# Sparse attention by pairs of heads with the values stationary, and additions to x one tile ahead

## What is computed

```python
def mixer_b(h, w_in, q_gain, k_gain, w_out, bias_tab):
    q, k, v, q_idx, k_idx, w_idx = split_last(h @ w_in, B_SPLITS)
    q = rms_norm(q.reshape(B, S, B_HEADS, HEAD_DIM), q_gain)
    k = rms_norm(k.reshape(B, S, B_KV_HEADS, HEAD_DIM), k_gain)
...
        sc = jnp.einsum('bqhd,bsd->bqhs', qib, k_idx).astype(jnp.float32) * (B_IDX_DIM ** -0.5)
        score = jnp.einsum('bqh,bqhs->bqs', wb.astype(jnp.float32), jax.nn.relu(sc))
        score = jnp.where(causal[None], score, -jnp.inf)
        _, sel = lax.top_k(score, topk)
...
        logits = jnp.einsum('bqhgd,bqkhd->bqhgk', qg, ks).astype(jnp.float32) * (HEAD_DIM ** -0.5)
        logits = jnp.where(valid[:, :, None, None, :], logits + bias, -jnp.inf)
        p = jax.nn.softmax(logits, axis=-1)
        o = jnp.einsum('bqhgk,bqkhd->bqhgd', p.astype(vs.dtype), vs)
...
    return out @ w_out
```

## Time and profile before

| | us |
|---|---|
| median of 3 runs | 3229.18 (3228.82 to 3231.17) |
| profiled execution | 3230.55 |
| its span | 3228.7 |
| PE busy | 3043.1 (94%) |
| DVE, ACT, POOL busy | 1073.0, 1108.9, 1371.6 |
| mean granted clock | 0.946 of full |

### The profile page before, as it was taken

The page is one execution under the profiler, slowest core; times in us unless marked ns, Lnnn a source line. Parts: engine busy times, 40 slices in busy tenths (PEclk is TensorE's granted clock), DMA queues, the critical chain, the costliest instruction groups (busy, mean ns, idle before and its releaser), DMA issues.

```text
span 3228.7 us, 37198 instructions
## 1 busy us (share of the span) xinstructions
PE 3043.1 (94%) x14352; PEld 2432.1 (75%) x14352; DVE 1073.0 (33%) x2072; ACT 1108.9 (34%) x1684; POOL 1371.6 (42%) x1097
## 2 busy tenths in 40 slices
PE   7999769999989989999899999899999999779999
PEld 5977558888656668888677787688888977558887
DVE  3023541113373341112656555311122133531112
ACT  4233432223343332223333434322334333332222
POOL 3455524454442224444433333244445355524443
PEclk8999889999985589999999999999999999889999
DMA  4222112323320012233311111122323222112332
GB/s 122 72 59 59 40 40 91 104 91 98 78 69 20 20 43 91 92 96 99 86 40 40 40 40 40 40 92 93 102 91 93 65 59 59 40 52 92 95 100 78
DMA packets 280064, 227.59 MB, mean 70 GB/s; under 512 B 30229, under 2 KB 275733, under 8 KB 279941
## 3 DMA queue, kind: packets, MB, share of 16 engines
q1 hardware_dynamic: 269200, 216.29, 22.4%
q10 hardware_dynamic: 10740, 9.65, 1.3%
HBM read 223.61 MB, written 2.30 MB: 70 GB/s over the span
## 4 chain that ended last, share of the span: by engine, by line
PE 83%; DVE 8%; POOL 4%; ACT 3%; issue 1%; DMA 0%; ACTq 0%; DVEq 0%; POOLq 0%
PE bank L1738 43%; PE bank L1681 22%; POOL w_lo L600 3%; PE bank L1758 3%; PE bank L1783 2%; PE bank L2081 1%; PE bank L2093 1%; PE bank L2090 1%; PE bank L1806 1%; PE bank L1771 1%; ACT w_hi L719 1%; POOL arena L622 1%; PE bank L1887 1%; PE bank L1905 1%; DVE rs L1327 1%
## 5 line engine op out<-in xcount | busy, mean ns | idle before, releaser
L600 POOL TENSOR_TENSOR w_lo<-raw,w_hi 128x512 fp32r<-128x512 f32 x808 | 1067.0, 1351 | 1385.4 <-ACT w_hi L719 1385.4
L719 ACT ACTIVATE w_hi<-raw 128x2048 fp32r<-128x2048 f32 x202 | 385.5, 1909 | 430.8 <-PE bank L1738 423.3
L1738 PE MATMUL bank<-h_hi,w_hi 128*128 128x512 f32 x1024 | 403.8, 394 | 0.0
L1738 PE MATMUL bank<-h_lo,w_hi 128*128 128x512 f32 x1024 | 400.7, 391 | 0.0
L1738 PE MATMUL bank<-h_hi,w_lo 128*128 128x512 f32 x1024 | 400.7, 391 | 0.0
L1738 PE MATMUL bank<-g_hi,w_hi 128*128 128x512 f32 x1024 | 398.3, 389 | 0.0
L1738 PE MATMUL bank<-g_lo,w_hi 128*128 128x512 f32 x1024 | 398.3, 389 | 0.0
L1738 PE MATMUL bank<-g_hi,w_lo 128*128 128x512 f32 x1024 | 398.3, 389 | 0.0
L1681 PE MATMUL bank<-h_hi,w_hi 128*128 128x512 f32 x784 | 339.7, 433 | 6.9 <-POOL w_lo L600 4.6
L1681 PE MATMUL bank<-h_lo,w_hi 128*128 128x512 f32 x784 | 316.7, 404 | 0.0
L1681 PE MATMUL bank<-h_hi,w_lo 128*128 128x512 f32 x784 | 316.3, 403 | 0.0
(11 more groups left out here) (245 smaller groups left out, 4591.7 us busy)
## 6 DMA issues: line engine op xcount, KB each, us to landing
raw<-in_mlp_w SPq DMA_DIRECT2D x128, 1024.0 KB, 5.3
raw<-in_a_w_in SPq DMA_DIRECT2D x48, 512.0 KB, 5.1
raw<-in_c_w_in SPq DMA_DIRECT2D x32, 512.0 KB, 5.6
raw<-in_a_w_in SPq DMA_DIRECT2D x12, 1024.0 KB, 5.0
raw<-in_b_w_in SPq DMA_DIRECT2D x18, 256.0 KB, 4.2
raw<-in_a_w_out SPq DMA_DIRECT2D x4, 1024.0 KB, 5.6
raw<-in_b_w_in SPq DMA_DIRECT2D x4, 1024.0 KB, 6.1
arena<-bias_scratch ACTq DMA_DIRECT2D x16, 256.0 KB, 3.1
```

Of the source, the lines that this page charges most:

```text
L600: ins = nc.gpsimd.tensor_tensor(w_lo[s][:, k, :], raw[s][:, k, :], w_hi[s][:, k, :].bitcast(F32), ALU.subtract)
L719: nc.scalar.activation(w_hi[s][:], raw[s][:], ACT.Copy).then_inc(w_hi_done, 1)
L1738: mm = nc.tensor.matmul(lin_bank[j][:], w[s][:, c, P * j:P * j + P], a[:, c, :], start=c + z == 0, stop=c == CT - 1 and z == 2)
```

## The change

In the sparse layer's attention a unit is now a block of queries for both heads of a pair: 32 units. The scores of the two heads use the two halves of the array's rows and banks 2 and 3; logits are negated, as in the dilated layers, so that one reduction gives the minimum and the exponential takes it as its bias. Transposes of the two heads go to banks 4 and 5, copied by ACT and DVE. In the weighing 64 columns of V are stationary and the probabilities stream, 128 columns at a time; bank 6 takes a whole pair, already transposed. The sums of a pair are inverted at once, spread over 64 partitions by eight matmuls with the identity, copied by ACT and multiplied in on DVE. Logits have four buffers, copied probabilities three. The scores of the next unit wait until both heads' logits of the last are done. POOL's mask additions take both heads at once.

The output projection is cut by heads: two chunks for the first eight heads, two for the others, four tiles of 12 matmuls in each. The first 96 matmuls run eight a step from step 21 on, 18 more in the two steps after the last unit. x so gets 16 additions instead of 8.

In the projections, keys come before queries, index scores are issued in twos, their relus have six buffers and the squares two, and the last five selection rounds stand behind the last addition of eps. In `residual` DVE adds tile c+1 to x before it makes the low part and the sum of tile c, in all layers.

```diff
+B_ORDER = (3, 0, 2, 1)
+B_UNITS = B_PAIRS * NB
+B_EARLY = (21, 8)
...
-            chunks += [("bq", i, c, CT, 4) for c in range(4)] + [("bk", i, 0, CT, 1)]
-            chunks += [("out", i, k, CT, 4) for k in range(4)]
+            chunks += [("bk", i, 0, CT, 1)] + [("bq", i, c, CT, 4) for c in range(4)]
+            chunks += [("bo", i, k, 4, 2) for k in range(4)]
...
+        bpt = [part(2 * TOK).rearrange("p (h n) -> p h n", h=2) for _ in range(3)]
+        btm = [part(2 * TOK).rearrange("p (h n) -> p h n", h=2) for _ in range(2)]
...
+        INDEX_AT = {(0, z): 2 * z for z in range(4)}
+        INDEX_AT.update({(2 + z // 2, 2 * (z % 2)): 8 + 2 * z for z in range(4)})
+        INDEX_AT.update({(6 + z // 2, 2 * (z % 2)): 16 + 2 * z for z in range(4)})
...
+            first, share = B_EARLY
+            return max(0, share * (s - first)), max(0, min(96, share * (s - first + 1)))
...
+                    t, n = b_masked(u), P * (b + 1)
...
+                    if t >= 2:
+                        pool.wait_ge(l_done, 2 * (4 * ((t - 2) // 3) + (0, 2, 3)[(t - 2) % 3] + 1))
+                    nc.gpsimd.tensor_tensor(btm[t % 2][:, :, 0:n], bbias[f % 2][:, :, TOK - n:TOK],
+                                            score[b].unsqueeze(1).to_broadcast([P, 2, n]), ALU.add).then_inc(tm_done, 1)
...
+                for u in range(B_UNITS):
+                    f, z, b = b_unit(u)
+                    if b:
+                        masked(u)
+                    for n in (chunk_at["bo", i, 0], chunk_at["bo", i, 1]):
+                        if u >= 2 and any(t + 1 == tile0[n + 1] for _, t in b_ended(i, u - 2)):
+                            split_ahead(n)
...
+                def probs(u):
+                    f, z, b = b_unit(u)
+                    for half in range(2):
+                        act.wait_ge(l_done, 2 * u + half + 1)
+                        t = bl[u % 4][:, half, 0:P * (b + 1)]
+                        c = 2 * b + half
+                        nc.scalar.activation(t, t, ACT.Exp, bias=b_stat(f, 0)[:, c:c + 1], scale=-1.0,
+                                             accum_out=b_stat(f, 1)[:, c:c + 1]).then_inc(p_done, 1)
...
+                def copy_turned(u):
+                    n = P * (b_unit(u)[2] + 1)
+                    act.wait_ge(pt_done, 2 * u + 1)
+                    if u >= 3:
+                        act.wait_ge(pv_done, u - 2)
+                    nc.scalar.activation(bpt[u % 3][:, 0, 0:n], bank[4][:, 0:n], ACT.Copy).then_inc(pt_copied[0], 1)
...
+                for s in range(B_UNITS + 6):
+                    f, z = divmod(s, NB)
+                    if 2 <= s < B_UNITS + 2:
+                        copy_turned(s - 2)
+                    if s < B_UNITS:
+                        if z == 1 and 1 <= f < B_PAIRS - 1:
+                            load_bias(f + 1)
+                        probs(s)
+                    if z == 2 and f:
+                        act.wait_ge(rinv_spread, f)
+                        act.wait_ge(y_done, f - 1) if f > 1 else act.wait_ge(qk_ready, Q + 10)
+                        nc.scalar.activation(brs, stat_bank[:], ACT.Copy).then_inc(rinv_copied, 1)
+                    if z == 3 and f:
+                        act.wait_ge(y_done, f)
+                        nc.scalar.activation(g_hi[:, f - 1, :], byf, ACT.Copy).then_inc(yh_done, 1)
+                    for n, t in b_ended(i, s - 1):
+                        if t + 1 == tile0[n + 1]:
+                            round_ahead(n)
...
-                for c in range(CT):
-                    dve.wait_ge(lin_done, t0 + c + 1)
-                    nc.vector.tensor_tensor(x[:, c, :], x[:, c, :], lin_bank[(t0 + c) % 2][:], ALU.add).then_inc(x_added, 1)
-                    if m is not None:
-                        dve.wait_ge(x_added, x0 + c + 1)
-                        low_x(m, c)
-                        sum_square(m, c)
+                for c in range(CT + 1):
+                    if c < CT:
+                        dve.wait_ge(lin_done, t0 + c + 1)
+                        nc.vector.tensor_tensor(x[:, c, :], x[:, c, :], lin_bank[(t0 + c) % 2][:],
+                                                ALU.add).then_inc(x_added, 1)
+                    if m is not None and c:
+                        dve.wait_ge(x_added, x0 + c)
+                        low_x(m, c - 1)
...
+                def logits(u):
+                    f, z, b = b_unit(u)
+                    n = P * (b + 1)
...
+                    if b:
+                        dve.wait_ge(tm_done, b_masked(u) + 1)
+                    else:
+                        dve.wait_ge(bbias_loaded[f % 2], 32 * (f // 2 + 1))
+                    dve.wait_ge(s_done, u + 1)
+                    for half in range(2):
+                        bias = btm[b_masked(u) % 2][:, half, 0:n] if b else bbias[f % 2][:, half, TOK - n:TOK]
+                        c = 2 * b + half
+                        nc.vector.tensor_tensor_reduce(
+                            out=bl[u % 4][:, half, 0:n], in0=bank[2 + half][:, 0:n], in1=bias, scale=1.0,
+                            scalar=-TAKEN, op0=ALU.add, op1=ALU.min,
+                            accum_out=b_stat(f, 0)[:, c:c + 1]).then_inc(l_done, 1)
...
+                    dve.wait_ge(p_done, 8 * f + 8)
+                    nc.vector.reciprocal(b_stat(f, 2), b_stat(f, 1)).then_inc(rinv_done, 1)
...
+                def outputs(f):
+                    dve.wait_ge(pv_done, 4 * f + 4)
+                    dve.wait_ge(rinv_copied, f + 1)
+                    nc.vector.tensor_tensor(by_block(byf), reversed_blocks(bank[6][:]), reversed_blocks(brs),
+                                            ALU.mult).then_inc(y_done, 1)
...
+                index_sums(range(8))
+                beside = {2: ((3, 0, 7),), 3: ((3, 7, 11),), 4: ((3, 11, 15),), 5: ((3, 15, 16),), 6: ((2, 0, 5),),
+                          7: ((2, 5, 10),), 8: ((2, 10, 14),), 9: ((2, 14, 16), (1, 0, 1)), 10: ((1, 1, 6),),
+                          11: ((1, 6, 11),)}
+                for k in range(2, 12):
+                    for b, lo, hi in beside[k]:
+                        if (b, lo) == (1, 0):
+                            index_sums(range(20, 24))
+                        for r in range(lo, hi):
+                            top(b, (r,))
+                    if k in (2, 5, 7):
+                        p = {2: 8, 5: 12, 7: 16}[k]
+                        index_sums(range(p, p + 4))
+                    add_eps(1, Q + k - 2, k >= 4)
+                top(1, range(11, 16))
...
+                for s in range(B_UNITS + 6):
+                    f, z = divmod(s, NB)
+                    if z == 3 and f:
+                        outputs(f - 1)
+                    if s < B_UNITS:
+                        logits(s)
+                    if 2 <= s < B_UNITS + 2:
+                        copy_turned(s - 2)
+                    if z == 0 and 0 < f <= B_PAIRS:
+                        inverses(f - 1)
+                    if z == 0 and f >= 2:
+                        low(f - 2)
+                    for n, t in b_ended(i, s):
+                        j = t - tile0[chunk_at["bo", i, 0]]
+                        dve.wait_ge(lin_done, t + 1)
+                        nc.vector.tensor_tensor(x[:, j, :], x[:, j, :], lin_bank[t % 2][:], ALU.add).then_inc(x_added, 1)
 
...
+                def scores(u):
+                    f, z, b = b_unit(u)
+                    if u:
+                        pe.wait_ge(l_done, 2 * u)
+                    for half in range(2):
+                        r = slice(HD * half, HD * half + HD)
+                        mm = nc.tensor.matmul(bank[2 + half][:, 0:P * (b + 1)], bq[f][r, P * b:P * b + P],
+                                              bk[f // 4][r, 0:P * (b + 1)], start=True, stop=True)
+                    mm.then_inc(s_done, 1)
+                def turn(u):
+                    b = b_unit(u)[2]
+                    for half in range(2):
+                        pe.wait_ge(p_done, 2 * u + half + 1)
+                        if u:
+                            pe.wait_ge(pt_copied[half], u)
+                        for k in range(b + 1):
+                            c = slice(P * k, P * k + P)
+                            mm = nc.tensor.transpose(bank[4 + half][:, c], bl[u % 4][:, half, c], ident)
+                        mm.then_inc(pt_done, 1)
+                def weigh(u):
+                    f, z, b = b_unit(u)
+                    if u == 0:
+                        pe.wait_ge(copied, copy_first[i] + 8)
+                    if z == 0 and f:
+                        pe.wait_ge(y_done, f)
+                    for half in range(2):
+                        pe.wait_ge(pt_copied[half], u + 1)
+                    for k in range(b + 1):
+                        for half in range(2):
+                            c = (2 * (f // 4) + half) * HD
+                            mm = nc.tensor.matmul(bank[6][HD * half:HD * half + HD, P * b:P * b + P], bv[:, k, c:c + HD],
```

(33 more changed lines are left out.)

470 lines of the change are left out of this document (133 added, 337 removed).

## The result

The changed kernel takes 3088.1 us in the median (3086.1 to 3091.7), against 3229.0 for the kernel before: a ratio of 0.9564, 95% interval 0.9547 to 0.9580, or 141 us less. The profiled execution took 3086.1 us with a span of 3084.3. The forecast was 3086, with a range of 3066 to 3120. From one profiled execution to the other it is 144.4 us, where -144 was forecast.

The account below looks back on a forecast made before the run. The prediction took TensorE's own instruction stream at half clock in the sparse layer's attention as the bound. Attention -116, projections -16, additions to x -13 and +1 sum to -144 us, from 3230.55 to 3086; range 3066 to 3120.

Parts of the forecast that it names:

- The price of a pair: Sparse attention: a pair of heads takes 8.7 us of TensorE work plus two waits at full clock, 11.0 us.
- The sum of 4.75 us for the outputs: Sparse attention: chain before bank 6 is free takes 4.75 us, TensorE arrives at 3.15, so 1.6 us lost a pair.
- The clock: Sparse attention: both array halves streaming bring full clock from about step 5 of 32; five start-up steps take 15.6 us.
- rival 1: Sparse attention: clock stays at half until the output products come at step 21; +25 us, 3111; chance 0.09.
- Rival 2: Sparse attention: the two heads do not overlap on TensorE, so streams double; +30 us, 3116; chance 0.04.
- rival 3: Sparse attention: handovers between engines set the pace, 3.5 us a step instead of 2.75; +20 us, 3106; chance 0.08.
- rival 4: Sparse attention: each unit's chain ends before the next begins and gaps keep half clock; slower than before, 3250; chance 0.02.
- The range's upper term: Sparse attention: 0.6 us more wait in each of 34 steps plus a 4.92 us weight split, given as 23 us more.
- Projections: Ahead of sparse attention: paired index scores save 10 us and selection starts earlier; -16 us, between -4 and -19.
- Additions to x: Two dilated layers' last projections: adding one tile ahead gives -6.9 us each, less 0.8; -13 us, -10 to -17.
- The recurrent layer's +1: Recurrent layer: the last sum comes 0.5 us later and is not hidden; +1 us.
- POOL's slack: Sparse attention: POOL's doubled-width mask additions, about 2.5 us for 512 columns, stay hidden by 0.5 us in the steady state.

## Why the prediction was right

**What bounds the stage.** Right. PE was busy 98% of the stage at a clock of 0.50, and edits of TensorE's stream alone (scores on one half, old weighing) give back 50 of the 116 us. The other 66 are not taken apart; most of them, by the estimate above, are the clock.

**The price of a pair.** 11.0 forecast, 11.05 measured, but by two errors that cancel. Work: scores 1.06 + 0.85 + 0.64 + 0.42 = 2.97 (3.0 forecast), weighing 1.02 + 0.75 + 0.59 + 0.43 = 2.8 (2.7), spreading 0.93 (0.85), transposes 0.81 + 0.58 + 1.02 + 0.44 = 2.85, where the step with 20 x 0.41/4 = 2.1 took its price from transposes that products follow; ahead of weighing or spreading four of them take 0.58. So 9.5 instead of 8.7. Waits: 0.38 for logits and 1.13 for outputs, 1.5 instead of 2.25. That the two errors, 0.8 each way, cancel is luck. (The sum of 4.75 us for the outputs had 0.18 left for handovers, of which that chain has several at 0.15; by its own terms the wait should have been forecast longer still.) That the second hangs on the order of ACT and DVE is shown: with the copy and the multiplication earlier it is gone.

**The clock.** Right in its result: up 9.7 us after the first scores (in step 3, where step 5 was said), and it stayed up without products, so rival 1 fell. The reason given, both halves streaming, is only part of it. It rose ahead of the first weighing, so the new weighing didn't raise it. With the scores side by side it was up after 9.5 to 9.7 us in all three forms of the weighing; with the scores on one half after 16, 30 and 54 us, and there the weighing counts. Old weighing and scores one at a time together hold it down longest, and still not for 184 us. What held it in the old kernel stays open. The fall was misread too: the trace has the clock down from 950.06, within the idle stretch ahead of 954.20 and not at its end; no term rests on that. Rival 2 fell (1.06 against 1.91 us for the widest scores), rival 3 too (3.5 us a step were not reached), rival 4 with them.

**Stage by stage.** Start-up 13.9 us (15.6 forecast, the clock came earlier), sixteen steps 44.2 (44), twelve steps with products 51.9 (52), the last two 7.4 (7.5), the last pair's outputs, said to be hidden by nine products, 0.9 late (0.3), 78 products 18.2 (17.8), tail 4.0 (3.4; in some of the tiles DVE's low part takes 1.18 us and its sum 1.78, instead of 0.75 and 0.68, with POOL busy beside them). Sum 140.5 against 140.6. The range's upper term, 0.6 x 34 + 4.92, is 25.3 and not 23, which changes nothing here.

**Projections.** -14.4 instead of -16. Only 10 of the 16 had a price of their own, so the closeness shows little. The 938 us given for the first scores was 954.2 - 16 and left out what comes from ahead of the layer, 8.2 us up to its norm; hence 931.61. The wait of 6.81 us in front of them is the split on POOL, which the prediction said would stay; moving it gave 3.8 us. The waits for additions of eps, of which two new ones were forecast, are three as before, 3.4 us together instead of 5.4; the last is the 1.41 us at 923.68.

**Additions to x.** -12.6 us in the kernel before alone, for -13 + 1 forecast. Per dilated layer the stretch gives 5.4 us, not 6.9: additions 1.86 us apart are as priced, but the first two tiles wait for TensorE, and the 0.8 set aside for both layers was too little. 1.8 us came from the clock instead. The recurrent layer's +1 did not show (-0.1).

**The sum.** From trace to trace: attention -115.8 (-116 forecast), projections -14.4 (-16), the two dilated layers -11.9 (-13), the recurrent layer -0.1 (+1), and 2.2 us less in the feed-forwards, the start and the end that no term had. Together -144.4 for -144: the total is closer than its parts.

**What was mis-sized and didn't matter.** POOL's slack, 0.5 us forecast, is 2.3 by the timeline (the addition for a pair's widest unit is done 2.3 us before its logits) and 1.6 by the doubled addition. By the prediction's number the doubled addition would have cost 13 us or more; it cost 8.3, with the clock's relapse in it.

## What to carry over

Where a stage shows PE busy all the time at half clock, count its stream at both clocks and try it with both halves of the array in use, before looking for waits. Price a form of instruction by what follows it: the same transposes cost 0.41 us ahead of products and 0.58 ahead of 64-column weights. And compare kernels by the stage that was changed, not by the total alone: a stage elsewhere can give back or add 4 us through the clock.

## What the runs showed of the hardware

- Out of the same start (gaps of 1.5 and 0.7 us in the first 7 us after the first scores, then none of more than 0.12 us up to the rise) the clock came up after 9.7, 9.5 and 9.5 us with the scores on both halves and the weighing new, one head at a time, and old; with the scores on one half after 16, 30 and 54 us. PE's busy share doesn't tell a low clock from a full one (51.5 of 53.9 us at 0.50; 38.2 of 44.2 at 1.00). It can also fall without a long gap: with the old weighing it fell 1.4 us after a gap of 0.88 us, and with the scores on one half as well 2.3 us after one of 0.46, though the changed kernel kept it over gaps of 1.13 us in every pair.
- Around the same idle stretch of 4.68 us the clock was at half for 3.4 us in one run and for 13.7 in another. The code is the same; when the stage begins is not.
- Weighing with 64 columns stationary, eight products: 1.51 us in head order, 1.02 interleaved; six: 1.02 and 0.75; four: 0.59 in both. The sizes fit an overlap at the seam between the heads alone, which is inferred.
- A DVE addition of 512 columns with both operands in SBUF took 1.75 us beside POOL's weight split and 0.69 alone.
